# Stick-breaking phase of a streaming encoder: one of VectorE's two copies of turned weights goes to ScalarE

## What is computed

```python
def stick_breaking(q, k, v, q_pos, k_pos):
    z = jnp.einsum('bqhd,bshd->bhqs', q, k).astype(jnp.float32) * (d ** -0.5)
    causal = (k_pos[None, :] < q_pos[:, None])[None, None]
    log_beta = jax.nn.log_sigmoid(z)
    log_rest = jnp.where(causal, jax.nn.log_sigmoid(-z), 0.0)
    suffix = lax.cumsum(log_rest, axis=3, reverse=True) - log_rest
    A = jnp.where(causal, jnp.exp(log_beta + suffix), 0.0)
    return jnp.einsum('bhqs,bshd->bqhd', A.astype(v.dtype), v)
```

## Time and profile before

| | |
|---|---|
| median of three runs | 3097.01 us |
| the profiled execution, its own time | 3091.68 us |
| span of the profiled execution | 3090.0 us |
| TensorE matmuls busy | 2896.4 us (94%) |
| VectorE busy | 1513.3 us (49%) |
| ScalarE busy | 1004.6 us (33%) |
| GpSimd busy | 1147.8 us (37%) |
| mean granted TensorE clock | 0.975 of full |

### The profile page before, as it was taken

How to read it: one execution, slowest core, us unless ns; L and a number is a source line. 1 busy time by engine, 2 the same in 40 slices (tenths; PEclk the granted TensorE clock), 3 DMA queues, 4 the chain that set the end, 5 groups by cost and what they waited for, 6 DMA issues and landing times. The chain is left out here.

```text
span 3090.0 us, 50524 instructions
## 1 busy us (share of the span) xinstructions
PE 2896.4 (94%) x20331; PEld 2384.9 (77%) x20331; DVE 1513.3 (49%) x2135; ACT 1004.6 (33%) x1843; POOL 1147.8 (37%) x1001
## 2 busy tenths in 40 slices
PE   6899999999989999989998999899988996999798
PEld 5788888888877888867776777677766776877686
DVE  7232221100004777666766676567657774333333
ACT  6441211111113444434443444334435662000221
POOL 4242331111104445445544545345535563433100
PEclk9899999999999999999999999999998998999899
DMA  6543332212216554665466545754448348444443
GB/s 215 178 154 114 131 123 68 79 68 71 73 66 215 171 162 156 223 214 176 159 215 217 185 159 175 240 189 159 150 153 229 126 128 238 165 169 163 163 143 109
DMA packets 383015, 485.98 MB, mean 157 GB/s; under 512 B 27888, under 2 KB 241904, under 8 KB 382416
## 3 DMA queue, kind: packets, MB, share of 16 engines
q1 hardware_dynamic: 341200, 359.32, 36.9%
q0 software_dynamic: 34688, 111.05, 9.6%
q10 hardware_dynamic: 6912, 12.59, 1.2%
HBM read 359.28 MB, written 123.60 MB: 156 GB/s over the span
## 5 line engine op out<-in xcount | busy, mean ns | idle before, releaser
L376 PE MATMUL prj_bank<-hidden_hi,w_hi 128*128 128x512 f32 (+2 forms) x1360 | 490.9, 361 | 13.1 <-DVE w_lo L439 13.1
L378 PE MATMUL prj_bank<-hidden_hi,w_lo 128*128 128x512 f32 (+2 forms) x1360 | 487.1, 358 | 0.0
L377 PE MATMUL prj_bank<-hidden_lo,w_hi 128*128 128x512 f32 (+2 forms) x1360 | 486.8, 358 | 0.0
L1100 POOL TENSOR_TENSOR stk_beta<-stk_beta,stk_left 128x1024 f32<-128x1024 f32 (+4 forms) x160 | 275.8, 1724 | 549.2 <-DVE stk_left L1017 549.2
L809 PE MATMUL stk_g_bank<-hidden_hi,w_hi 128*128 128x512 f32 (+2 forms) x928 | 351.1, 378 | 14.6 <-PEq L62 10.8
L811 PE MATMUL stk_g_bank<-hidden_hi,w_lo 128*128 128x512 f32 (+2 forms) x928 | 336.6, 363 | 0.0
L810 PE MATMUL stk_g_bank<-hidden_lo,w_hi 128*128 128x512 f32 (+2 forms) x928 | 335.8, 362 | 0.0
L376 PEld LDWEIGHTS prj_bank<-hidden_hi,w_hi 128*128 128x128 f32 x1360 | 256.9, 189 | 44.8 <-DVE w_lo L439 13.3
L378 PEld LDWEIGHTS prj_bank<-hidden_hi,w_lo 128*128 128x128 f32 x1360 | 256.7, 189 | 32.5
L377 PEld LDWEIGHTS prj_bank<-hidden_lo,w_hi 128*128 128x128 f32 x1360 | 257.0, 189 | 31.3
L1017 DVE TENSOR_TENSOR_SCAN stk_left<-stk_rest,stk_left 128x513 f32<-128x513 f32 x192 | 244.6, 1314 | 8.1 <-ACT stk_rest L965 8.0
(11 more groups left out here) (254 smaller groups left out, 5460.2 us busy)
## 6 DMA issues: line engine op xcount, KB each, us to landing
stk_kd<-in_cache_sb_k SPq DMA_DIRECT2D x64, 1024.0 KB, 5.4
stk_vd<-in_cache_sb_v SPq DMA_DIRECT2D x64, 1024.0 KB, 7.3
w_raw<-in_w_in SPq DMA_DIRECT2D x112, 512.0 KB, 3.8
scratch_zT<-stk_g_out POOLq DMA_DIRECT2D x72, 256.0 KB, 2.3
mrg_gate<-scratch_zT SPq DMA_DIRECT2D x24, 768.0 KB, 4.4
scratch_zT<-prj_z POOLq DMA_DIRECT2D x48, 256.0 KB, 2.3
prj_w<-in_w_in SPq DMA_DIRECT2D x18, 512.0 KB, 3.9
mrg_u_raw<-scratch_uT SPq DMA_DIRECT2D x9, 1024.0 KB, 9.2
```

Source lines behind the costliest of these rows:

```text
L376: pe.matmul(out, w_hi[u][:, k, :], hi[:, k, :], start=k == 0, stop=False)
L377: pe.matmul(out, w_hi[u][:, k, :], lo[:, k, :], start=False, stop=False)
L378: last = pe.matmul(out, w_lo[u][:, k, :], hi[:, k, :], start=False, stop=k == KC - 1)
L1100: pool.tensor_tensor(bt, bt, left[prompts.index(n) % 2][:, :, 1:keys + 1], ALU.mult).then_inc(a_done, 1)
```

## The change

VectorE's `copy_a` keeps only the first piece. A new `copy_a` on ScalarE copies the second piece; it runs after sigmoids(s), and where step s also has key copies, between the two. The semaphore of the second piece, `a_copied[1]`, is now raised by ScalarE; TensorE's waits are as before.

```diff
-            def copy_k(n):
+            def copy_k(n, c):
                 i = kblocks.index(n)
                 if i:
                     act.wait_ge(z_done, kblocks[i - 1] + 1)
                 else:
                     act.wait_ge(masks, 3)
-                for c in (1, 3):
-                    act.wait_ge(kd_turned, 4 * i + c + 1)
-                    act.activation(kd_t[:, c, :], z[n % 2][:, 1, :], ACT.Copy).then_inc(kd_copied[1], 1)
+                act.wait_ge(kd_turned, 4 * i + c + 1)
+                act.activation(kd_t[:, c, :], z[n % 2][:, 1, :], ACT.Copy).then_inc(kd_copied[1], 1)
+
+            def copy_a(n):
+
+                cols = width(n) if units[n][1] == "p" else width(n) // 2
+                wait(act, o_added, n - 1)
+                act.wait_ge(a_turned[1], with_two(n))
+                act.activation(a_t[n % 2][:, 1, 0:cols], turn_bank[:, 1, 0:cols], ACT.Copy).then_inc(a_copied[1], 1)
...
                 if s + 1 in kblocks:
-                    copy_k(s + 1)
+                    copy_k(s + 1, 1)
+                if 0 <= s - LAG_T < N and pieces[s - LAG_T] == 2:
+                    copy_a(s - LAG_T)
+                if s + 1 in kblocks:
+                    copy_k(s + 1, 3)
...
                 keys, cols = (DT, P) if w == DT else (P, w if prompt else w // 2)
-                for p in range(pieces[n]):
-                    dve.wait_ge(a_turned[p], n + 1 if p == 0 else with_two(n))
-                    dve.tensor_copy(a_t[n % 2][0:keys, p, 0:cols], turn_bank[0:keys, p, 0:cols]).then_inc(a_copied[p], 1)
+                dve.wait_ge(a_turned[0], n + 1)
+                dve.tensor_copy(a_t[n % 2][0:keys, 0, 0:cols], turn_bank[0:keys, 0, 0:cols]).then_inc(a_copied[0], 1)
```

## The result

| | median | runs | lowest to highest |
|---|---|---|---|
| before | 3095.54 us | 20 | 3089.05 to 3104.75 |
| changed | 3103.14 us | 20 | 3098.32 to 3107.64 |

The ratio is 1.0026, with a 95% interval of 1.0018 to 1.0033: the change costs some 8 us. I had forecast 3096.0 in a range of 3087 to 3102.

The account below looks back on a forecast made before the run. TensorE was taken to bound the kernel, busy 1292.0 of 1337.0 us. Terms -1.9 - 0.6 + 1.6 = -0.9 us, on a median of 3097.0, gave 3096.0 us; own range 3091 to 3101, widened to 3087 to 3102.

Parts of the forecast that it names:

- The bound and the loads: Stick phase: TensorE bounds; 224 copies move, leaving ScalarE at 661 and VectorE at 808 of 1337 us.
- What the relief is worth: TensorE's waits ended by VectorE: at most 9.2 us to gain, credited with 1.9 because scans would still wait for GpSimd.
- The four waits that depend on who gets in first: Four TensorE waits behind scans meeting GpSimd's subtraction, 2.5 us together; earlier scans might win, a quarter credited: 0.6 us.
- the row at 1001.67: Profile row: a scan began 0.29 us ahead of the subtraction, yet two scans took 4.34 us instead of 1.9.
- What ScalarE's queue costs: Copies late behind ScalarE's earlier work: 1.6 us lost at the phase's start (third unit), 0 in the first gap.
- the gap: First of three gaps where ScalarE issues loads: scores begin 0.8 us late, but covered; taken as 0, bound 0.8.
- ScalarE's order: Slower rival: second copies wait behind everything holding ScalarE; a fifth of 50.8 us lost gives 3107 us; chance 0.14.
- The faster rival: Scans shift in GpSimd's rhythm, so VectorE's 24.5 us of waits shrink beyond the copies; 3088 or 3081 us; chance 0.27.
- larger means of scans and gate products: Sign on VectorE: scans and gate products begin earlier and wait for GpSimd, so their means rise; no size given.
- Key copies down by 1 to 3 us: Sign: TensorE's 14.7 us of waiting for VectorE's key copies falls by 1 to 3 us.
- theory B: Explanation tested in the follow-up runs: ScalarE, in order, is late with the copies it took over.
- TensorE's idle time below 38 us: Sign in the stick phase, where it was 45.0 us: falling below 38 would show the forecast wrong, the relief reaching TensorE.

Follow-up runs that it names:

- relief alone: The changed kernel without ScalarE's copies: nobody copies the second piece and TensorE does not wait for it; 3100.58 us, ratio 1.0014 to the kernel before.
- giving the held units back: The changed kernel with VectorE copying second pieces of the first three units and those behind ScalarE's 16 loads; 3101.96 us, ratio 1.0022 to the kernel before.

## Why the prediction was wrong, point by point

- **The bound and the loads**: right for TensorE and ScalarE. TensorE is the bound, ScalarE came to 652.7 us (forecast 661), its copy of 512 columns takes about 0.6 us, and laying the copies into the timeline was sound: TensorE waits for ScalarE's copy in two places of 224, and ScalarE's queue costs no time that the runs can tell. VectorE came to 873.6 us and not to the 808 forecast, for the reason of the next point.
- **What the relief is worth** (credited with -1.9 us): this is the step that failed. I had seen that scans wait for GpSimd, and concluded that starting a scan sooner can at worst end in waiting. I held GpSimd's instructions fixed while moving VectorE's. But the product follows the scans and the subtraction follows the product, so the subtraction comes earlier by the whole copy, while the next scan and gate product are tied to TensorE and come earlier by less or not at all. The relief's worth was not -1.9 but, by the run with the relief alone, about +4 us (1.5 to 7). That the loss hangs on the copies ahead of a subtraction, and is gone without the subtraction or with the gate product behind the copies, is what the other runs show.
- **The four waits that depend on who gets in first** (credited with -0.6 us): the question was the right one, but I asked it of the four scans that lost, and not of the 21 that won. Reading the row at 1001.67 as "0.29 us ahead is not enough" was right; the scans that had 0.56 us and were about to lose it were in the same trace. The Trainium skill's rule in "SBUF — State Buffer", section "Who interferes with whom", that the first to issue gets the pair for the whole instruction, agrees with scans and gate products being held for the full subtraction (3.99 and 3.00 us). By the recorded starts, "first" needs 0.56 us for the decode scan here.
- **What ScalarE's queue costs** (+1.6 us at the start, 0 in the gap): the gap was right, it has the new wait of 4.5 us in place of one for `rest` and loses nothing with it. At the start the second to fourth unit lost 0.8 us between them instead of 1.6, as VectorE was late there too.
- **The rivals**: the slower one that I named was ScalarE's order, with 0.14; the slower case came true by the other engine. The faster rival had the mechanism that did come true (scans in other places of GpSimd's rhythm), with the sign turned round: here the kernel stood on the good side of an edge.
- **The signs** I gave in advance: larger means of scans and gate products came true for the scans and were written off as harmless. Key copies down by 1 to 3 us: down by 0.7. TensorE's waits for ScalarE's copy over 8 us would have meant theory B: they are 4.8. TensorE's idle time below 38 us would have meant a gain: it rose to 49.6.
- **The sum** itself is added up right but for a rounding: 3097.0 - 0.9 is 3096.1 and not 3096.0.

ScalarE's own share stays open within about 4 us: relief alone is at 1.0014 (1.0005 to 1.0023), the change at 1.0026 (1.0018 to 1.0033), and giving the held units back changed nothing measurable.

## What to carry to other kernels

Before taking work off an engine, ask what its relief will let start earlier, follow that to the other engines, and check against which instruction each newcomer now runs; what is tied to the bounding engine does not move along, so gaps between the two shrink. Look at the pairs that get by each other narrowly, not only at those that collide: an instruction with two typical durations, like the decode scan before (1.27 or 3.6 us), names them. And where an instruction can be held by another engine, put nothing behind it that the bounding engine waits for soon: moving the gate product behind the copies was worth 12 us; moving half of the copies to a free engine cost 8 us, and with the gate product moved it was worth nothing.

## What the runs showed of the hardware that I had not expected

- A scan of 513 columns with both inputs in SBUF was spared by GpSimd's subtraction of 128x1024 where it started 0.56 us or more ahead by the recorded times; at 0.55 us or less it was held for the whole of it. Held scans of 1.27 us took up to 4.03 us. A gate product was spared with as little as 0.26 us in the changed kernel and held with 0.48: recorded starts this close do not say who is first.
- Each can hold the other: where the scan won, the subtraction took up to 2.90 instead of 2.39 us.
- Where one copy of 0.4 to 0.7 us had left the step before, the scan's start and the subtraction's came 0.26 us closer in most places (0.78 to 0.52 us, 0.56 to 0.30). That turned all 21 of these meetings from one side to the other, and VectorE waited 57 us more.
